# First matrices of the MLPs and the shared keys' first block loaded as two K-tiles by 512 columns, with four column blocks summed side by side in two banks

## What is computed

```python
def squared_relu_mlp(h, w1, w2):                 # h [256, 1024], w1 [1024, 4096], w2 [4096, 1024]
    return jnp.square(jax.nn.relu(h @ w1)) @ w2

mod = (c_act @ ada_w[layer] + ada_b[layer])[:, None, :]     # conditioning, [1024] @ [1024, 6144]
h = modulate(rms_norm(x, mlp_norm[layer]), sh_m, sc_m)
x = x + gt_m * squared_relu_mlp(h, mlp_w1[layer], mlp_w2[layer])
kv = (h_kv @ w_kv)                                # w_kv [1024, 1536]: its first 512 columns feed the compressed keys
```

## Time and profile before

| | |
|---|---|
| median of 3 executions | 1409.15 us (1406.42 to 1410.65) |
| profiled execution | 1413.62 us, span of its rows 1411.8 us |
| busy | TensorE 94%, VectorE 62%, ScalarE 48%, GpSimd 12% |
| granted TensorE clock | 0.972 of full over the span |
| first MLP and its start, 200 to 400 us | clock 1.00, TensorE busy 194.20, VectorE 164.12, DMA share 0.86, 289 GB/s |
| second MLP, 640 to 780 us | clock 1.00, TensorE busy 140.00, VectorE 69.07, DMA share 0.65, 194 GB/s |
| third MLP, 914 to 1115 us | clock 1.00, TensorE busy 200.59 of 201.00 |
| fourth MLP, 1228 to 1411 us | clock 1.00, TensorE busy 179.83 of 183.00 |

### The profile page before, as it was taken

How to read it: one execution, slowest core, us unless ns; L and a number is a source line. 1 busy time by engine, 2 the same in 40 slices (tenths; PEclk the granted TensorE clock), 3 DMA queues, 4 the chain that set the end, 5 groups by cost and what they waited for, 6 DMA issues and landing times.

```text
span 1411.8 us, 22238 instructions
## 1 busy us (share of the span) xinstructions
PE 1320.3 (94%) x8582; PEld 1140.6 (81%) x8582; DVE 872.8 (62%) x1546; ACT 679.5 (48%) x1196; POOL 171.2 (12%) x172
## 2 busy tenths in 40 slices
PE   6797999999999999999999878999999998899999
PEld 2687899888889855789898765799998776799987
DVE  2768578888667377695545675565555554645443
ACT  2454554343554346454445575554444555554442
POOL 0546011100100000010000130011010101011000
PEclk9889999999999899999999999999999999999999
DMA  9967639899868433269655262198655454376660
GB/s 350 314 219 241 193 105 311 301 312 341 298 185 229 146 120 91 82 196 281 189 182 158 87 191 61 61 229 251 182 177 180 134 180 119 102 203 184 184 179 31
DMA packets 249225, 267.43 MB, mean 189 GB/s; under 512 B 11040, under 2 KB 185376, under 8 KB 248736
## 3 DMA queue, kind: packets, MB, share of 16 engines
q1 hardware_dynamic: 246496, 263.52, 60.1%
q10 hardware_dynamic: 2624, 2.49, 0.5%
HBM read 264.83 MB, written 1.15 MB: 188 GB/s over the span
## 4 chain that ended last, share of the span: by engine, by line
PE 56%; DVE 7%; ACT 4%; issue 2%; POOL 1%; ACTq 0%; DMA 0%; DVEq 0%; POOLq 0%
PE bank L558 10%; PE bank L560 9%; PE bank L559 9%; PE ps_s L558 3%; PE ps_s L559 3%; PE ps_s L560 3%; PE ps_p L559 3%; PE ps_p L558 3%; PE ps_p L560 3%; DVE wlo L1564 2%; ACT whi L2661 2%; PE ps_s L1273 1%; POOL rs L3288 1%; PE ps_p L1139 1%; PE ps_s L1103 1%
## 5 line engine op out<-in xcount | busy, mean ns | idle before, releaser
L1564 DVE TENSOR_TENSOR wlo<-wring,whi 128x1024 fp32r<-128x1024 f32 (+1 forms) x376 | 456.2, 1229 | 231.0 <-ACT whi L2661 229.2
L2661 ACT ACTIVATE whi<-wring 128x1024 fp32r<-128x1024 f32 (+1 forms) x376 | 388.5, 1043 | 353.7 <-PE ps_p L560 123.2
L558 PE MATMUL bank<-h_hi,whi 128*128 128x256 f32 x1216 | 351.7, 289 | 4.7 <-DVE h_lo L1739 2.3
L559 PE MATMUL bank<-h_lo,whi 128*128 128x256 f32 x1216 | 347.8, 286 | 0.0
L560 PE MATMUL bank<-h_hi,wlo 128*128 128x256 f32 x1216 | 347.5, 286 | 0.0
L558 PEld LDWEIGHTS bank<-h_hi,whi 128*128 128x128 f32 x1216 | 237.3, 195 | 10.7 <-issue 7.4
L559 PEld LDWEIGHTS bank<-h_lo,whi 128*128 128x128 f32 x1216 | 237.3, 195 | 0.7
L560 PEld LDWEIGHTS bank<-h_hi,wlo 128*128 128x128 f32 x1216 | 237.1, 195 | 0.0
L3326 POOL TENSOR_TENSOR ex<-ex 128x512 f32<-128x512 f32 x64 | 72.4, 1131 | 714.3 <-ACT g_hi L2792 714.3
L1807 DVE TENSOR_TENSOR g_lo<-ex,g_hi 128x512 fp32r<-128x512 f32 x64 | 44.2, 690 | 125.9 <-POOL ex L3326 125.7
L558 PE MATMUL bank<-whi,h_hi 128*128 128x512 f32 (+3 forms) x248 | 100.5, 405 | 15.2 <-DVE h_lo L1685 6.2
(11 more groups left out here) (394 smaller groups left out, 1886.4 us busy)
## 6 DMA issues: line engine op xcount, KB each, us to landing
wring<-in_mlp_w SPq DMA_DIRECT2D x128, 512.0 KB, 5.2
wring<-in_ada_w SPq DMA_DIRECT2D x96, 512.0 KB, 7.2
wring<-in_mlp_w_in SPq DMA_DIRECT2D x64, 512.0 KB, 4.7
wring<-in_mlp_w_out SPq DMA_DIRECT2D x64, 512.0 KB, 4.1
wring<-in_a_w_in SPq DMA_DIRECT2D x24, 512.0 KB, 5.7
wring<-in_moba_w_qkv SPq DMA_DIRECT2D x24, 512.0 KB, 3.9
wring<-in_kv_ada_w SPq DMA_DIRECT2D x16, 512.0 KB, 7.6
wring<-in_w_kv SPq DMA_DIRECT2D x12, 512.0 KB, 5.2
```

The source lines that it names most:

```text
L558: nc.tensor.matmul(out, lh, rh, start=first, stop=False)
L559: nc.tensor.matmul(out, lh, rl, start=False, stop=False)
L1564: v.tensor_tensor(piece_view(wlo, p), raw_view(p), piece_view(whi, p).bitcast(F32), ALU.subtract).then_inc(lo_ready, 1)
L2661: a.activation(piece_view(whi, p), raw_view(p), ACT.Copy).then_inc(hi_ready, 1)
```

## The change

Three things are edited. The kinds of the w1 matrices and of the first block of w_kv go from "f" to "t". A new function `by_pairs` takes the place of `by_feature` for them: it takes both banks at the start, and for each piece (two K-tiles) runs all four column blocks of 128, six matmuls each, so that all four sums stay open over the four pieces; only the first matmul into a bank has the start flag. The first bank is full 12 matmuls before the second, and both count as ended by the last piece. And VectorE's `g_low` of a chunk's two halves moves from one step after the half's last piece to three and four steps after the chunk's last piece. The number of loads, their order and bytes, and the number and shapes of matmuls stay.

```diff
     def mlp(tag):
-        w1 = mat(f"{tag}_w1", D, FF, "f" * 8)
+        w1 = mat(f"{tag}_w1", D, FF, "t" * 8)
...
-    w_kv, b_in = mat("w_kv", D, 1536, ["f", "ft", "ft"]), mat("b_in", D, 1072, "fft")
+    w_kv, b_in = mat("w_kv", D, 1536, ["t", "ft", "ft"]), mat("b_in", D, 1072, "fft")
...
+            def by_pairs(key, src, ready=None):
+
+                banks = [bank_take(pe, key + (g,)) for g in range(2)]
+                for j in range(KT // 2):
+                    p = piece_wait()
+                    wh, wl = piece_view(whi, p), piece_view(wlo, p)
+                    for n in range(4):
+                        g, i = divmod(n, 2)
+                        for k in (2 * j, 2 * j + 1):
+                            if ready and n == 0:
+                                ready(k)
+                            at = (slice(None), k % 2, slice(n * P, (n + 1) * P))
+                            last = product(bank[:, banks[g], i * T:(i + 1) * T], (wh[at], wl[at]),
+                                           (src[0][:, k, :], src[1][:, k, :]), k == 0 and i == 0, k == KT - 1, True)
+                        if n == 1 and j == KT // 2 - 1:
+                            last.then_inc(filled[banks[0]], 1)
+                    piece_over(last, key + (1,) if j == KT // 2 - 1 else None)
+                for g in range(2):
+                    piece_of[key + (g,)] = p
...
                 def up(c):
-                    by_feature((f"{tag}_w1", c), (h_hi, h_lo), W, ready=(lambda k: wait(tag, k)) if c == 0 else None)
+                    by_pairs((f"{tag}_w1", c), (h_hi, h_lo), (lambda k: wait(tag, k)) if c == 0 else None)
...
-            by_feature(("w_kv", 0), h_kv, W, ready=lambda k: half_split("kv", k))
+            by_pairs(("w_kv", 0), h_kv, lambda k: half_split("kv", k))
...
-                late = None
+                due = {}
...
-                    if late is not None:
-                        g_low(late)
-                        late = None
+                    if j in due:
+                        g_low(due[j])
                     key = pieces[p][0]
-                    local = p - first_piece[key]
-                    if key[0].endswith("w1") and local % 2:
-                        late = 2 * key[1] + local // 2
+                    if key[0].endswith("w1") and p == first_piece[key] + 3:
+                        due.update({j + 3: 2 * key[1], j + 4: 2 * key[1] + 1})
```

More of the change, by code:

```diff
@@ L553, in _, with product @@
             n_read = [0]
-            def product(out, left, right, first, last):
+            def product(out, left, right, first, last, mixed=False):
                 (lh, ll), (rh, rl) = left, right
-                nc.tensor.matmul(out, lh, rh, start=first, stop=False)
-                nc.tensor.matmul(out, lh, rl, start=False, stop=False)
-                return nc.tensor.matmul(out, ll, rh, start=False, stop=last)
+                nc.tensor.matmul(out, lh, rh, start=first, stop=False, skip_group_check=mixed)
+                nc.tensor.matmul(out, lh, rl, start=False, stop=False, skip_group_check=mixed)
+                return nc.tensor.matmul(out, ll, rh, start=False, stop=last, skip_group_check=mixed)
             def by_feature(key, src, n, name=None, ready=None):
```

## The result

The changed kernel takes 1416.03 us (median of 20 runs, 1406.7 to 1419.95); the kernel before, measured beside it, 1410.63 (20 runs). The ratio is 1.0035, 95% interval 1.0021 to 1.0048: slower by a third of a per cent, where I had forecast 1407.1 and a range up to 1413.5. The profiled span grew from 1411.8 to 1416.0 us, by 4.2, and the mean granted clock fell from 0.972 to 0.967.

The account below looks back on a forecast made before the run. TensorE, busy 94% of the span, was taken as the bound, losing time in few places. The terms -7.6 + 0.2 + 4.1 + 2.3 - 1.0 = -2.0 us put the median at 1407.1 us, range 1402.5 to 1413.5.

Parts of the forecast that it names:

- Part 1: First MLP: wider w1 rows land the first w2 load 1.1 us earlier per round; with Part 2, -7.6 us.
- (b): Rival: row length is worth nothing, the first MLP gives 3.3 us; sum +2.3, 1411.5 us; chance 0.17.
- Part 2: First MLP, VectorE's queue: later g_low saves 0.65 us per round; -3.3 us if only this works.
- Part 3: First down block waits for chunk 0's later g_low: +0.2 us in the first MLP, +4.1 in the second.
- Part 4: Shared keys: the first bank is released later, so TensorE's next block starts +2.3 us later, all passed on.
- Part 5: First block of the third and fourth MLP: TensorE's wait at K-tile 4 goes, -1.0 us for both.
- (a): Rival: no new gate in the second MLP, key bank released in time; -11.3 us, 1397.9; chance 0.15.
- (c): Rival: the first MLP stays paced by VectorE, its 7.9 us loss stays; +5.6 us, 1414.8; chance 0.16.

Follow-up runs that it names:

- e9_warm_half: The changed kernel with 10, 7 and 19 small matmuls, results never read, in its three new waits: 1408.35 us, ratio 0.9968 to the kernel before.
- e4_long_rows: The kernel before with only w1 laid out in memory for 4 KB rows, order of work unchanged: 1400.92 us, ratio 0.9948.
- e7_short_rows: e1_gate with w1 laid out so that its loads come in rows of 512 bytes, not 2 KB: 1407.45 us, ratio 0.9973 to the kernel before.
- e1_gate: The changed kernel with only chunk 0's two g_low moved back to one and two steps after the chunk: 1405.96 us, ratio 0.9977 to the kernel before.
- e8_gate_alone: The kernel before with only g_low moved to three and four steps after the chunk's last piece: 1413.48 us, ratio 1.0006.
- e6_gateall: The changed kernel with all chunks' g_low at one and two steps after the chunk: 1406.20 us, ratio 0.9975 to the kernel before.
- e3_both: The changed kernel with chunk 0's g_low early and w_kv's first block as before: 1403.77 us, ratio 0.9945 to the kernel before.
- the last two kernels: e3_both with small matmuls ahead of three, then four, waits that the kernel before has too: 1398.27 and 1397.92 us, ratios 0.9916 and 0.9909.
- e2_kvf: The changed kernel with w_kv's first block again of kind "f" and by_feature: 1413.50 us, ratio 1.0031 to the kernel before.
- e5_warm: The changed kernel with 22, 14 and 40 small matmuls, results never read, in its three new waits: 1417.88 us, ratio 1.0039 to the kernel before.

## Why the prediction was wrong

**The step that failed** is the price of a wait, in parts 3 and 4: "Its weights are then ready, so the next up block starts 11.82 later" and "+2.3 us ... all of it is passed on". I priced each wait at its own length and the block behind it at full clock. What stands behind them runs at 0.50 for 3 to 5 us: 1.6 us lost in the first MLP's down block (13.43 against 11.82), 2.3 in the second's (14.15 against 11.82), 2.6 in the shared keys' next block (8.45 against 5.85). That is 6.5 us, and e9_warm_half, which gets 6.2 us back with the waits left in place, shows it by experiment; without it the span would have shrunk by 2.3, where I forecast 2.0. That this comes so near is in part luck, since the other errors cancel: +1.4 at the first gate, -1.2 at the second, -1.3 ahead of the first MLP and +1.4 in the sparse attention. The last is read from windows alone: both kernels wait 2.1 us near 501 us, and only in the changed kernel's trace the clock falls behind it. No run ties that to the change, and the stretch varies by more between traces of the same instructions.

**Part 1, right in size; the cause shared.** -7.6 was forecast, -7.9 and 0.6 at the end of the stage came. Rival (b), row length worth nothing, is refuted in its mechanism by e4_long_rows (-5.7 us in the four rounds, -0.52% of the time). But e7_short_rows shows that most of this edit's gain doesn't hang on it: order and late `g_low` together give 5.5 without it. ScalarE waited for the weights 48.3 us after the change, against 83.2; that number misled, since it is 74.2 in e1_gate with the same rounds. In the changed kernel ScalarE waits more for TensorE's pieces (44.2 us, 18.8 in e1_gate) in place of the DMA.

**Part 2, right alone, worth nothing beside the rest.** The late `g_low` gives 4.8 us by itself (e8_gate_alone), more than my bound of 3.3, and nothing once rows and order are changed (e6_gateall). I had added it to part 1 and cut the sum at the 7.9 that were there to lose; the cut is what made the number right, and that was luck as far as the two parts go.

**Part 3, the waits foreseen, both sizes off.** First MLP: forecast +0.2, bound +0.9; the down block comes 25.49 us behind the first up block and not 23.92, +1.6, and the clock adds 1.6. Second MLP: forecast 30.4 us from the first up block to the down block, measured 29.20. VectorE's rows in the changed kernel, in order of time, the first MLP's two on top:

```profile
218.89 1.23 DVE L1584 TENSOR_TENSOR wlo<-wring,whi 128x1024 fp32r<-128x1024 f32 x1 [0.73 <-ACT whi L2679]
...
223.22 1.53 DVE L1827 TENSOR_TENSOR g_lo<-ex,g_hi 128x512 fp32r<-128x512 f32 x1
...
611.10 3.10 DVE L1603 SCALAR_TENSOR_TENSOR acc<-wring,c_col,acc 128x512 f32<-128x512 f32 x3
614.12 2.06 DVE L1584 TENSOR_TENSOR wlo<-wring,whi 128x1024 fp32r<-128x1024 f32 x1
...
617.54 1.22 DVE L1584 TENSOR_TENSOR wlo<-wring,whi 128x1024 fp32r<-128x1024 f32 x1
...
629.36 0.68 DVE L1827 TENSOR_TENSOR g_lo<-ex,g_hi 128x512 fp32r<-128x512 f32 x1
```

In the first MLP the gating `g_low` itself is held up by a square, 1.53 us for 0.68, and VectorE waits 0.73 us for ScalarE's split; my bound of +0.9 had neither. In the second the two squares of chunk 0 hold up the conditioning step (3.10 us for the 2.40 of before) and one split (2.06 for 1.22), 1.5 us together and not the 2.1 that I counted. The other 0.6 of the difference is that VectorE gets to this point 0.6 us sooner (610.58, not 611.18): before, the first half's square fell into the attention layer's last operations. This row of the kernel before is 1.00 us long after the change:

```profile
607.81 1.73 DVE L2311 SCALAR_TENSOR_TENSOR att<-att 128x64 f32<-128x64 f32 x4
```

e1_gate shows that the gate alone makes both waits: with it early neither is there.

**Part 4, the wait exact.** From the late down piece to TensorE's next block it is 25.99 us after and 23.73 before: +2.26 for the forecast +2.3. Of the other 3.0 us 2.6 are the slow block behind it, and the last 0.4 come where TensorE waits for VectorE near 454 us.

**Part 5, right in kind, a little more than its bound of -1.1.** The wait at K-tile 4 is gone; from first up to first down block the third MLP takes 23.10 us and not 23.78, the fourth 23.10 and not 23.77: -1.35 for the forecast -1.0.

**Rivals.** (a) is refuted by the waits; (c) by the rounds of 24.23 us, in which TensorE never waits. The kernel ended on (c)'s side, and near its 1414.8, for another reason, that none of the three held.

## What to carry to other kernels

Price a new wait of TensorE at its length plus the clock behind it. Waits of about 2 us and less brought the clock down in some traces and not in others, so below that the price has two values. Where it fell behind the new waits, it was 0.50 for 3 to 5 us, which cost 1.6 to 2.6 us, as much again as waits of 1.4 and 2.4 us and over half of one of 4.2. Look for the granted clock beside each wait that the kernel already has. Where such a wait can't be removed, small matmuls into a bank that is free, sized by their measured duration to end just before the wait does, got that part back (0.7% in the changed kernel; between e3_both and the last two kernels the ratios differ by 0.3 to 0.4%, with intervals that overlap a little, and one of their fills gained nothing, as the clock fell again further on). Follow the clock to the end of the stage, not only behind the fill. Several cures of one stall don't add: cap their sum by the stall, and test each alone before one is credited.

## What the runs showed of the hardware beyond that

- A wait of 1.42 us was enough to bring the clock to 0.50 (224.80), and so were 1.84 us of one-column products (e2_kvf). Waits of 2.10 us near 501 us and of 1.70 at 358.91 in the kernel before were not, nor were the same products in it. Which waits do it differs between kernels whose instructions there are the same; only what ran earlier differs. From the second MLP's end to the third MLP e1_gate takes 129.6 us and e7_short_rows 126.7 with the same instructions, the latter without the slow stretch behind head 4's turn. So single traces can differ by 3 us in a stage that no edit touched. What decides it no run here settles.
- A 128-column float32 matmul of the identity is two rows of 0.11 us (80 rows for 40 instructions in e5_warm).
- A subtraction of 128 by 512 on VectorE takes 0.68 us and took 1.53 (changed kernel, above) and 1.57 (e8_gate_alone) while GpSimd squared, as the split takes 2.06 for 1.22.
